# Merging weights held on 64 partitions, GpSimd gate products, and fewer, merged instructions for a decay attention's levels

## The reference, cut to what matters

```python
wts = jax.nn.softmax(jnp.stack(lses), axis=0)
o = jnp.sum(wts[..., None] * jnp.stack(outs).astype(jnp.float32), axis=0)
o = o.reshape(B, S, ATTN_WIDTH).astype(h.dtype)
return (o * jax.nn.silu(z)) @ w_out
```

```python
G = jnp.cumsum(g_, axis=2)
diff = G[:, :, :, None, :] - G[:, :, None, :, :]
decay = jnp.exp(jnp.where(causal[:, :, None], diff, -jnp.inf))
A = jnp.einsum('bhtk,bhsk,bhtsk->bhts', q_, k_, decay)
```

## Time and profile before

| what | us |
|---|---|
| median of 3 runs (4005.82 to 4010.16) | 4006.62 |
| the profiled execution's own time | 4003.77 |
| its span, first to last instruction | 4002.0 |
| stage A, from its barrier at 607.2 to the next stage's first matmul at 683.96 | 76.8 |
| stage B, from 1981.8 to the next stage's first matmul at 2181.97 | 200.2 |
| PE busy over the whole span | 3653.1 (91%) |
| DVE, ACT, POOL busy over the whole span | 1691.3, 896.4, 1905.6 |

### The profile page before, as it was taken

One profiled execution on the slowest core, in us unless ns is written; L12 is line 12 of the kernel. 1 busy time (PEld: TensorE's weight loads), 2 busy tenths in 40 slices (PEclk: granted clock), 3 DMA queues, 4 the chain that ended last, 5 costly groups with the idle time before them and its releaser, 6 DMA issues. The chain is left out here.

```text
span 4002.0 us, 47523 instructions
## 1 busy us (share of the span) xinstructions
PE 3653.1 (91%) x18444; PEld 2985.3 (75%) x18444; DVE 1691.3 (42%) x2710; ACT 896.4 (22%) x2349; POOL 1905.6 (48%) x749
## 2 busy tenths in 40 slices
PE   8999996798888899999966999998999998889999
PEld 6787873677776788878756888876888877678887
DVE  5523236887366422144375411337411236642213
ACT  2333332222134211111132100126100023421111
POOL 5444430523532365555643555651566553236554
PEclk9999995887999899999988999998999999889999
DMA  4236861243221222222201222230222222122221
GB/s 139 85 128 92 111 98 54 68 120 87 91 74 64 79 95 96 102 86 91 82 1 37 86 102 96 93 107 27 107 95 94 95 96 74 64 79 95 96 102 76
DMA packets 96530, 346.75 MB, mean 87 GB/s; under 512 B 27270, under 2 KB 45958, under 8 KB 61528
## 3 DMA queue, kind: packets, MB, share of 16 engines
q1 hardware_dynamic: 83984, 318.45, 26.6%
q10 hardware_dynamic: 12360, 25.70, 1.9%
HBM read 321.04 MB, written 18.87 MB: 85 GB/s over the span
## 5 line engine op out<-in xcount | busy, mean ns | idle before, releaser
L294 POOL CAST wh<-raw 128x2048 fp32r<-128x2048 f32 x269 | 512.8, 1906 | 1670.0 <-PE bank L336 1273.3
L296 POOL TENSOR_TENSOR wl<-raw,wh 128x2048 fp32r<-128x2048 f32 x269 | 1245.9, 4632 | 21.5
L334 PE MATMUL bank<-XTh,wh 128*128 128x512 f32 (+1 forms) x2448 | 951.1, 389 | 45.0 <-DVE XTl L1167 15.1
L336 PE MATMUL bank<-XTl,wh 128*128 128x512 f32 (+1 forms) x2448 | 935.3, 382 | 0.0
L335 PE MATMUL bank<-XTh,wl 128*128 128x512 f32 (+1 forms) x2448 | 934.7, 382 | 0.0
L334 PEld LDWEIGHTS bank<-XTh,wh 128*128 128x128 f32 x2448 | 467.5, 191 | 155.5 <-issue 41.8
L336 PEld LDWEIGHTS bank<-XTl,wh 128*128 128x128 f32 x2448 | 465.8, 190 | 89.8
L335 PEld LDWEIGHTS bank<-XTh,wl 128*128 128x128 f32 x2448 | 468.0, 191 | 84.6
L334 PE MATMUL bank<-wh,XTh 128*128 128x512 f32 (+2 forms) x1056 | 392.8, 372 | 37.9 <-DVE XTl L1167 12.6
L335 PE MATMUL bank<-wh,HTl 128*128 128x512 f32 x1024 | 403.4, 394 | 0.0
L334 PE MATMUL bank<-wh,HTh 128*128 128x512 f32 x1024 | 401.7, 392 | 0.0
(11 more groups left out here) (355 smaller groups left out, 4035.6 us busy)
## 6 DMA issues: line engine op xcount, KB each, us to landing
raw<-in_weights SPq DMA_DIRECT2D x270, 1024.0 KB, 4.8
B<-bias_d ACTq DMA_DIRECT2D x8, 1024.0 KB, 5.7
B<-bias_a ACTq DMA_DIRECT2D x8, 512.0 KB, 11.9
bias_d<-O SPq DMA_DIRECT2D x16, 256.0 KB, 21.3
MO<-HS SPq DMA_DIRECT2D x64, 64.0 KB, 2.8
bc<-in_ln_g ACTq DMA_DIRECT2D x8, 512.0 KB, 6.7
bc<-in_ln_b ACTq DMA_DIRECT2D x8, 512.0 KB, 7.1
X<-in_x SPq DMA_DIRECT2D x4, 512.0 KB, 7.9
```

Source lines behind the costliest of these rows:

```text
L294: pool.tensor_copy(wh[s][:, :], raw[r][:, :]).then_inc(w_high.h, 1)
L296: pool.tensor_tensor(wl[s][:, :], raw[r][:, :], wh[s][:, :].bitcast(F32), ALU.subtract).then_inc(w_split.h, 1)
L334: nc.tensor.matmul(psum, sh, mh, start=first, stop=False)
L336: return nc.tensor.matmul(psum, sh, ml, start=False, stop=last)
```

## The change

In stage A, `LR` gets 64 rows instead of 16: row 4h + j holds head h for the 128 tokens whose number is j modulo 4. Groups 1 and 2 lie so already, and take one transpose each. For group 0, DVE masks the logarithms by the partition modulo 4 (`picked`) and PE multiplies them with a constant matrix of ones (`quarter`), 4 matmuls of 64x32; DVE copies all in one instruction. The softmax then works on rows of 128 instead of 512. To spread the weights in the loop, DVE multiplies the reciprocal with the mask (`spread`) and each group with that (`share`, 64x512, one for each group); PE starts group 0 when the first is there. `sel` has 64 rows, and a small constant `quarters` is loaded ahead of it. In the loop, `acc` has two halves used in turn, the three banks of a tile are handed over one by one and come free after the third product, and the low part of tile p-1 is made behind tile p. The eight sigmoids run in one go on ACT, and POOL multiplies each with z, in place in `YF` (L2117 of the changed kernel); DVE then has one product with `YF` instead of two.

In stage B, tiles 0 and 2 are no longer made by POOL: ACT takes their exponentials from `LF` with the subtrahend as a bias, in 4 instructions of 128x128 (tile 0) and 8 of 128x64 (tile 2); `middles`, made once at the start, holds the negated biases. POOL keeps 6 subtractions per head. `KIN` and `QF` become parts of one tensor `KQ`, and a level's two multiplications become one of 128x512, whose second operand jumps between the key and query parts from half block to half block.

The core of the diff:

```diff
-    m = np.zeros((HEADS, 8, P), np.float32)
+    m = np.zeros((4 * HEADS, 8, P), np.float32)
...
+def quarters():
+
+    p = np.arange(P)[:, None]
+    return np.concatenate([p // 4 == np.arange(32), p % 4 == np.arange(4)], axis=1).astype(np.float32)
...
+                        sp.dma_start(quarter[:, :], t["quarters"]).then_inc(loaded.h, 16)
+                        sp.dma_start(sel[:, :, :], t["head_select"]).then_inc(selectors.h, 16)
+
+                    @block.gpsimd
+                    def _(pool):
+                        for p in range(8):
+                            pool.wait_ge(a_b.h, a_b.base + 3 + p)
+                            nc.gpsimd.tensor_tensor(YF[:, p, :], YF[:, p, :], sg[:, p, :], ALU.mult).then_inc(gated.h, 1)
...
                         for p in range(8):
-                            if p >= 2:
-                                act.wait_ge(tile2_free.h, tile2_free.base + p - 1)
-                            a.activation(sg[:, p % 2, :], YF[:, p, :], ACT.Sigmoid).then_inc(a_b.h, 1)
+                            a.activation(sg[:, p, :], YF[:, p, :], ACT.Sigmoid).then_inc(a_b.h, 1)
+                        for p in range(8):
                             act.wait_ge(b_a.h, b_a.base + 2 + p)
-                            a.activation(XTh[:, p, :], acc[:, 0, :], ACT.Copy).then_inc(a_p.h, 1)
+                            a.activation(XTh[:, p, :], acc[:, p % 2, :], ACT.Copy).then_inc(a_p.h, 1)
...
-                        for s in range(12):
-                            r = nc.tensor.transpose(PS[s // 4][0:HEADS, P * (s % 4):P * (s % 4) + P], SM[:, :, s], ident[:, :])
+                        for g in (1, 2):
+                            nc.tensor.transpose(PS[0][0:4 * HEADS, P * g:P * g + P], logs[:, g, :, :], ident[:, :])
+                        for tt in range(TT):
+                            r = nc.tensor.matmul(PS[0][0:4 * HEADS, 32 * tt:32 * tt + 32], picked[:, tt, :, :], quarter[:, 0:32], start=True, stop=True)
...
-                                r = nc.tensor.matmul(PS[4 * (p % 2) + g][:, :], sel[:, p, :], LR[:, g, :], start=True, stop=True)
-                            r.then_inc(p_b.h, 1)
+                                if p == 0:
+                                    pe.wait_ge(b_p.h, b_p.base + 2 + g)
+                                nc.tensor.matmul(PS[1 + 3 * (p % 2) + g][:, :], sel[:, p, :], share[:, g, :, :], start=True, stop=True).then_inc(p_b.h, 1)
...
                         for p in range(8):
...
+                            x = acc[:, p % 2, :]
+                            link(weigh(p, 0, x))
+                            link(weigh(p, 1, part[:, 0, :]))
+                            link(v.tensor_tensor(x, x, part[:, 0, :], ALU.add))
+                            link(weigh(p, 2, part[:, 1, :]))
+                            dve.sem_inc(tile2_free.h, 1)
+                            link(v.tensor_tensor(x, x, part[:, 1, :], ALU.add))
+                            dve.wait_ge(gated.h, gated.base + p + 1)
+                            v.tensor_tensor(x, x, YF[:, p, :], ALU.mult).then_inc(b_a.h, 1)
+
+                            if p:
+                                low(p - 1)
+                        low(7)
...
-                                for n in [0] + list(range(2, 9)):
+                                for n in range(3, 9):
...
-                                        r = a.activation(x, x, ACT.Exp)
+                                        g = of(LF, i, b)
+                                        for cc in range(TT):
+                                            cs = slice(P * cc, P * cc + P)
+                                            r = a.activation(x[:, cs], g[:, cs], ACT.Exp, scale=-1.0, bias=g[:, P * cc + P - 1:P * cc + P])
+                                    elif n == 2:
+                                        g, half = of(LF, i, b), P // 2
+                                        for cc in range(TT):
+                                            lo, mid = P * cc, P * cc + half
+                                            a.activation(x[:, lo:mid], g[:, lo:mid], ACT.Exp, scale=-1.0, bias=g[:, mid - 1:mid])
+                                            r = a.activation(x[:, mid:lo + P], g[:, mid:lo + P], ACT.Exp, bias=middles[:, 2 * i + b, cc:cc + 1])
...
-                                        link(v.tensor_tensor(x3[:, :, 0:half], x3[:, :, 0:half], kin[:, :, 0:half], ALU.mult))
-                                        v.tensor_tensor(x3[:, :, half:], x3[:, :, half:], q[:, :, half:], ALU.mult).then_inc(DW.h, 1)
+                                        half, k = P >> (n - 1), KIN[:, 2 * i + b, :]
+                                        x4 = x.rearrange("p (n y c) -> p n y c", y=2, c=half)
+                                        kq = bass.AP(k.tensor, k.offset, [list(k.ap[0]), [2 * half, S // (2 * half)], [KT * S + half, 2], [1, half]])
+                                        v.tensor_tensor(x4, x4, kq, ALU.mult).then_inc(DW.h, 1)
```

97 lines of the change are left out of this document (50 added, 47 removed).

## The result

The changed kernel takes **3962.4 us** (median of 4; 3956.6 to 3965.3) against 4006.2 before (median of 4; 4002.8 to 4010.2): ratio 0.9889, with a 95% interval from 0.9871 to 0.9906, so 38 to 52 us less, 44 by the medians. The forecast was 3971, 35 us less.

The account below looks back on a forecast made before the run. The prediction took the chain inside each changed stage, not PE's 91% busy time, as the bound. Stage A's 20.2 us plus stage B's 15 made 35 us, from 4006.62 to 3971 us; range 3965 to 3978 (0.70), wider 3962 to 3982.

Parts of the forecast that it names:

- Stage A, preparation: Stage A up to PE's first spreading matmul: PE starts at 617.8 instead of 626.28, 8.5 us less (7.5 to 9.6).
- Stage A, loop: Stage A from PE's first spreading matmul: PE (45.4 us) and DVE (45.2) come out level; stage 20.2 us shorter.
- two meetings: Stage A's loop, DVE instructions held up by POOL's gate products: three meetings of 0.5 us on average forecast, 1.5 us.
- Stage B, levels: Stage B, a head's middle piece, first merge through tile 7's multiplication: five levels take 4.0 instead of 6.0 us.
- Stage B, first head: First of stage B's eight heads, where PE is cold and late anyway: 1 us less.
- Stage B, first piece and tail: Stage B, a head before its first merge and after tile 7's multiplication: no gain counted there.
- POOL's disturbances as an amount: Stage B's levels: POOL's remaining instructions still cost DVE 0.9 us a head.
- ACT's 64.0 us of waiting: Stage B: ACT waits 8 us a head, so its small instructions (3.3 us a head instead of 1.5) stand behind that.
- PE's clock as a cause of a small gain: Rival: PE's clock stays at 1.2 GHz through stage B's levels, which gives 4 us: 3982; chance 0.12.
- Nothing meets: Rival: no DVE-POOL meetings left in stage B, 22 us gained in place of 15: 3964; chance 0.07.
- the slower rival: Rival: stage B's merged multiplication pays for its jumping operand, 2.2 us instead of 0.69: 4041; chance 0.03.
- The sum: Whole kernel: 20.2 us from stage A plus 15 from stage B, 35 us less, giving 3971 us.

Follow-up runs that it names:

- x4: Changed kernel, but each level multiplied in two halves as before; tiles 0 and 2 stay on ACT (POOL relieved only): 3979.3 us.
- x3: Changed kernel, but POOL makes all 64 subtractions of stage B and ACT the exponentials as before (merging only): 3958.0 us.
- y2: Changed kernel with all eight differences on POOL, tile 9's exponential before the turned head's copy, low part moved into next head, gate products behind the shares: 3936.2 us.

## Why the prediction fell short

- **Stage A, preparation: right.** The reading of ACT's table load was off: it ends 1.3 us behind the exponential, before and after, not 1.8; the first gate product starts 2.0 us behind it, as forecast. PE starts 10.71 us behind the first DMA (forecast 10.6). `picked` didn't wait (the chain runs from 613.44 to 614.32 without a gap); the reciprocal takes 0.94; the first share is held up by POOL.
- **Stage A, loop: right.** PE is busy without a gap at clock 0.50, a DVE tile is 5.07 us (forecast 5.05), two meetings cost about 1.7. The stage is 19.8 us shorter, forecast 20.2.
- **Stage B, levels: right for the head that was read, size too small, mechanism half right.** 2.0 us were forecast a head from 10.95 in the third head, to 8.95. The changed kernel has 8.94. But the other heads before took 11.1 to 12.5, and the mean over three executions with the old code is 11.2: 2.25 us a head, 1.8 more for the seven. That DVE loses time where POOL is ahead of it is right. That it pays less when POOL has less to do holds only for the two halves (10.5 instead of 11.2 in x4). Merging with all eight differences left on POOL has 8.18 (x3), so in the changed kernel the merging brings the gain and the relief takes part of it back. That 8.95 was met to the hundredth is therefore in part luck.
- **Stage B, first head: wrong, the step that failed most.** Forecast 1 us, "where PE is cold and late anyway". It went from 20.7 (also the mean of the three old executions) to 16.5, 4.3 us less, of which 0.9 are paid ahead of it by the later first product: 2.4 more than forecast. In that head DVE waited only 1.1 us for PE ahead of its merges before. It's bound by DVE and POOL: its levels went from 11.0 (the mean of the three) to 7.7, its tail from 6.2 to 5.1. By x3 and x4 merging alone takes 2.8 us off the head, relief alone 3.5, of which again 0.9 are paid ahead of it. Those 0.9 us, too, are more than the 0.5 forecast for `middles` and the small instructions.
- **Stage B, first piece and tail: taken as unchanged.** Against the three old executions they moved by -0.1 and +0.2 us a head. That the relief has a price was not seen: on top of merging the first piece grows by 0.8 us a head. The prediction took POOL's disturbances as an amount (0.9 us left of the levels) where one of them is a matter of which engine starts first, and it read ACT's 64.0 us of waiting as cover, though the exponential that DVE waits for in every tail stands behind that very wait.
- **The rivals.** PE's clock as a cause of a small gain didn't come about as the rival put it, but PE's clock does lengthen heads: in y2, with the same code, from 17.4 to 19.3 us. "Nothing meets" had the time (3964 against 3962.4) by luck, not the mechanism: one multiplication of 1.40 us is left in each of heads 2 to 7. The merged multiplication takes 0.68 to 0.75 us at tiles 2 to 7 of the undisturbed last head and 0.84 at tile 8, where it changes the tensor at each element, so the slower rival (2.2 us) is refuted.
- **The sum.** 19.8 + 19.1 (stage B against the mean of three old executions) are 39 us, within the measured 38 to 52; the forecast's 35 is short by 2.4 for the first head and 1.8 for the levels, and 0.4 too high in stage A. What is left up to 44 can't be told from the spread of the untouched stretches.
